# Attention scores, transposes and value products issued for two heads at a time

## Time and profile before

| | |
|---|---|
| median of 3 runs | 2915.23 us (2912.63 to 2915.69) |
| profiled execution | 2915.05 us |
| its span, first to last instruction | 2912.9 us |
| mean granted TensorE clock | 0.971 of full speed |
| busy: PE, PEld, DVE, ACT, POOL | 95%, 75%, 48%, 22%, 31% |

### The profile page before, as it was taken

One profiled execution on the slowest core, in us unless ns is written; L12 is line 12 of the kernel. 1 busy time (PEld: TensorE's weight loads), 2 busy tenths in 40 slices (PEclk: granted clock), 3 DMA queues, 4 the chain that ended last, 5 costly groups with the idle time before them and its releaser, 6 DMA issues.

```text
span 2912.9 us, 33971 instructions
## 1 busy us (share of the span) xinstructions
PE 2759.7 (95%) x12436; PEld 2198.0 (75%) x12436; DVE 1386.1 (48%) x2569; ACT 627.4 (22%) x1495; POOL 897.2 (31%) x870
## 2 busy tenths in 40 slices
PE   6799999999999999877999989998999999999997
PEld 2487778987789877765778767776787888888886
DVE  1421245986667676564346432223545344344346
ACT  3212222112321122441014022222122101101102
POOL 0531122432224232222424322222323343343343
PEclk8899999999999999997999989999999999999999
DMA  5410111122212132453334122223422111111113
GB/s 174 131 51 26 57 55 58 56 66 75 84 54 73 49 98 84 158 165 122 100 111 148 30 67 65 59 65 127 130 94 98 44 50 50 43 51 50 43 54 126
DMA packets 155596, 236.10 MB, mean 81 GB/s; under 512 B 24764, under 2 KB 69564, under 8 KB 155464
## 3 DMA queue, kind: packets, MB, share of 16 engines
q1 hardware_dynamic: 155464, 234.35, 25.3%
HBM read 181.65 MB, written 52.64 MB: 80 GB/s over the span
## 4 chain that ended last, share of the span: by engine, by line
PE 87%; DVE 8%; DMA 3%; ACT 1%; issue 1%; POOL 0%; SPq 0%; POOLq 0%; ACTq 0%; DVEq 0%
PE ps L1748 50%; PE ps L1895 12%; PE ps L1927 11%; PE ps L1806 5%; PE ps L1816 3%; PE ps L1830 3%; PE ps L1760 2%; PE ps L1777 2%; DVE act_lo L1239 1%; DVE scr L1326 1%; DMA small<-st_d 1%; DMA scr<-in_x 1%; DVE scr L1429 0%; DVE big L1669 0%; DVE big L1519 0%
## 5 line engine op out<-in xcount | busy, mean ns | idle before, releaser
L870 POOL CAST w_hi<-raw 128x512 fp32r<-128x512 f32 x416 | 306.0, 736 | 1948.5 <-DMA raw<-in_w_in 938.3
L1748 PE MATMUL ps<-act_hi,w_hi 128*128 128x512 f32 x1344 | 557.6, 415 | 48.4 <-DVE act_lo L1239 46.2
L872 POOL TENSOR_TENSOR w_lo<-raw,w_hi 128x512 fp32r<-128x512 f32 x416 | 580.3, 1395 | 33.3
L1748 PE MATMUL ps<-act_lo,w_hi 128*128 128x512 f32 x1344 | 532.6, 396 | 0.0
L1748 PE MATMUL ps<-act_hi,w_lo 128*128 128x512 f32 x1344 | 530.2, 394 | 0.0
L1326 DVE SCALAR_TENSOR_TENSOR scr<-scr,small 128x512 f32<-128x512 f32 x480 | 421.0, 877 | 11.5
L1748 PE MATMUL ps<-w_hi,act_hi 128*128 128x512 f32 (+1 forms) x960 | 387.4, 404 | 6.8 <-DVE act_lo L1239 6.5
L1748 PE MATMUL ps<-w_hi,act_lo 128*128 128x512 f32 (+1 forms) x960 | 376.0, 392 | 0.0
L1748 PE MATMUL ps<-w_lo,act_hi 128*128 128x512 f32 (+1 forms) x960 | 375.8, 391 | 0.0
L1748 PEld LDWEIGHTS ps<-act_hi,w_hi 128*128 128x128 f32 x1344 | 256.4, 191 | 102.2 <-issue 54.3
L1748 PEld LDWEIGHTS ps<-act_lo,w_hi 128*128 128x128 f32 x1344 | 255.6, 190 | 57.6
(11 more groups left out here) (173 smaller groups left out, 3113.5 us busy)
## 6 DMA issues: line engine op xcount, KB each, us to landing
raw<-in_w_in SPq DMA_DIRECT2D x176, 256.0 KB, 3.1
raw<-in_w_up SPq DMA_DIRECT2D x64, 256.0 KB, 2.7
raw<-in_w_down SPq DMA_DIRECT2D x64, 256.0 KB, 2.6
vreg<-in_w_ada SPq DMA_DIRECT2D x48, 256.0 KB, 3.5
raw<-in_w_in SPq DMA_DIRECT2D x72, 128.0 KB, 2.2
x_d<-big SPq DMA_DIRECT2D x16, 512.0 KB, 3.0
scr<-x_d SPq DMA_DIRECT2D x16, 512.0 KB, 4.2
o_d<-scr SPq DMA_DIRECT2D x48, 128.0 KB, 1.9
```

The source lines that it names most:

```text
L870: pool.tensor_copy(dhi, src).then_inc(w_hi_done, 1)
L872: pool.tensor_tensor(dlo, src, dhi.bitcast(F32), ALU.subtract).then_inc(w_ready, 1)
L1748: ins = nc.tensor.matmul(out_, lhs, rhs, start=(m == 0), stop=(m == 3 * nk - 1))
```

## The change

Two heads form a pair: heads 2i and 2i+1 of a block in groups 0 to 2, heads i and i+4 in group 3, always one on partitions 0 to 63 and one on 64 to 127. A group has 32 pairs and each does all its work within its own share of projection matmuls, 18 or 24 of them: 2 (3 in group 3) matmuls, both scores, 12 (15), all transposes of the pair into one bank, 4 (6), all value products of the pair into one bank. ScalarE copies the transposed probabilities of both heads in one instruction into the one buffer `probT`, VectorE both outputs in one. Counts of `probs_t`, `pt_out`, `pv` and `o_out` go by pairs. The taps of both steps come behind each other on VectorE, after both maxima. The cut diff (SyncE's two counts are halved alike; in group 3 VectorE's small steps for the sink, once a block, are put at pairs instead of steps):

```diff
+def pair_fill(C, p):
+
+    per = att_share(C)
+    a, b = 2 * p * per, 2 * p * per + 2 * per
+    return a, a + 2 * per // 8, b - 2 * per // 4, b
+
+
+def units_in(a, b):
+
+    return range(a // 24, b // 24)
+
-        probT = [scr[:, 512 + i * 256:512 + (i + 1) * 256] for i in range(2)]
+        probT = scr[:, 512:1024]
+        def pair_heads(g, p):
+
+            i = p % 4
+            return (2 * i, 2 * i + 1) if g < NG else (i, i + 4)
...
-            def probs_out(g, s):
-
-                a = 64 * g + s
-                n = att_cfg(g, s // 8)[1]
-                act.wait_ge(probs_t, a + 1)
-                if a >= 2:
-                    act.wait_ge(pv, a - 1)
-                nc.scalar.activation(probT[a % 2][:, 0:n], ps_t[:, 0:n], ACT.Copy
-                                     ).then_inc(pt_out, 1)
+            def probs_out(g, p):
+
+                n = att_cfg(g, p // 4)[1]
+                act.wait_ge(probs_t, 32 * g + p + 1)
+                if 32 * g + p >= 1:
+                    act.wait_ge(pv, 32 * g + p)
+                both = lambda t: t.rearrange("p (j k) -> p j k", j=2)[:, :, 0:n]
+                nc.scalar.activation(both(probT), both(ps_t), ACT.Copy).then_inc(pt_out, 1)
+
+            def att_pair(g, p):
+                us = att_units(g)
+                a, b, c, d = pair_fill(len(ATT_STAGES[g]), p)
+                for i in units_in(a, b):
+                    f_unit(us[i])
+                for j in range(2):
+                    exps(g, p, j)
+                for i in units_in(b, c):
+                    f_unit(us[i])
+                probs_out(g, p)
+                for i in units_in(c, d):
+                    f_unit(us[i])
...
-                B, h = s // 8, s % 8
+            def score_max(g, p, j):
+
+                B, h = p // 4, pair_heads(g, p)[j]
                 _, n, mask = att_cfg(g, B)
-                dve.wait_ge(scores, a + 1)
-                if a >= 2:
-                    dve.wait_ge(probs_t, a - 1)
-                nc.vector.tensor_tensor_reduce(prob[a % 2][:, 0:n], ps_s[a % 2][:, 0:n], mask, -0.125,
+                dve.wait_ge(scores, 64 * g + 2 * p + j + 1)
+                if 32 * g + p >= 1:
+                    dve.wait_ge(probs_t, 32 * g + p)
+                nc.vector.tensor_tensor_reduce(prob[j][:, 0:n], ps_s[j][:, 0:n], mask, -0.125,
                                                c_ns[:, h:h + 1] if g == 3 else 1e30, ALU.add, ALU.min,
                                                stat[:, B, h:h + 1]).then_inc(att_max, 1)
 
...
+            def out_pair(g, p):
+                B, i, a = p // 4, p % 4, 32 * g + p
                 dve.wait_ge(pv, a + 1)
-                src = ps_o[:, 0:HD]
+                src = ps_o[:, 0:2 * HD]
                 if g == 3:
-                nc.vector.tensor_copy(obuf[quad % 2][:, 64 * (h % 4):64 * (h % 4) + 64], src).then_inc(o_out, 1)
+                nc.vector.tensor_copy(obuf[quad % 2][:, P * (i % 2):P * (i % 2) + P], src).then_inc(o_out, 1)
...
             def attention(g):
                 us, C = att_units(g), len(ATT_STAGES[g])
                 if g >= 1:
                     dve.wait_ge(stat_st, 16 * (1, 3)[g - 1])
-                for s in range(66):
-                    if s < 64:
-                        score_max(g, s)
-                    if s >= 2:
-                        out_head(g, s - 2)
-                    if s < 64:
-                        for i in units_done(C, s):
-                            f_unit(us[i])
-                        if g < NG:
-                            conv_taps(("step", g, s))
+                for p in range(32):
+                    a, b, c, d = pair_fill(C, p)
+                    for i in units_in(a, b):
+                        f_unit(us[i])
+                    if p >= 1:
+                        out_pair(g, p - 1)
+                    for j in range(2):
+                        score_max(g, p, j)
+                    for i in units_in(b, d):
+                        f_unit(us[i])
+                    conv_taps(("step", g, 2 * p))
+                    conv_taps(("step", g, 2 * p + 1))
+                out_pair(g, 31)
...
-            def score(g, s):
-                a = 64 * g + s
-                B, h = s // 8, s % 8
+            def score_pair(g, p):
+                B = p // 4
                 k0, n, _ = att_cfg(g, B)
-                pair, half = (h // 2, h % 2) if g < 3 else (h % 4, h // 4)
-                rows = slice(64 * half, 64 * half + 64)
-                if a >= 2:
-                    pe.wait_ge(att_max, a - 1)
-                keys = kT[rows, pair, k0:k0 + n] if g < 3 else kT2[rows, k0:k0 + n]
-                nc.tensor.matmul(ps_s[a % 2][:, 0:n], qT[rows, pair, P * B:P * B + P], keys, start=True, stop=True
-                                 ).then_inc(scores, 1)
-
-            def prob_t(g, s):
-                a = 64 * g + s
-                n = att_cfg(g, s // 8)[1]
-                pe.wait_ge(probs, a + 1)
-                if a >= 1:
-                    pe.wait_ge(pt_out, a)
-                for i in range(n // P):
-                    ins = nc.tensor.transpose(ps_t[:, P * i:P * i + P],
-                                              prob[a % 2][:, P * i:P * i + P], ident[:, :])
+                if 32 * g + p >= 1:
+                    pe.wait_ge(att_max, 64 * g + 2 * p)
+                for j in range(2):
+                    rows = slice(64 * j, 64 * j + 64)
+                    keys = kT[rows, p % 4, k0:k0 + n] if g < 3 else kT2[rows, k0:k0 + n]
+                    nc.tensor.matmul(ps_s[j][:, 0:n], qT[rows, p % 4, P * B:P * B + P], keys, start=True, stop=True
+                                     ).then_inc(scores, 1)
+
+            def turn_pair(g, p):
+                n = att_cfg(g, p // 4)[1]
+                pe.wait_ge(probs, 64 * g + 2 * p + 2)
+                if 32 * g + p >= 1:
+                    pe.wait_ge(pt_out, 32 * g + p)
+                for j in range(2):
+                    for i in range(n // P):
+                        ins = nc.tensor.transpose(ps_t[:, 256 * j + P * i:256 * j + P * i + P],
+                                                  prob[j][:, P * i:P * i + P], ident[:, :])
                 ins.then_inc(probs_t, 1)
 
-            def prob_v(g, s):
-                a = 64 * g + s
-                B, h = s // 8, s % 8
-                k0, n, _ = att_cfg(g, B)
-                pe.wait_ge(pt_out, a + 1)
-                if a >= 1:
-                    pe.wait_ge(o_out, a)
-                for i in range(n // P):
-                    v = (V[:, k0 // P + i, 64 * h:64 * h + 64] if g < 3
-                         else V2[:, k0 // P + i, 64 * (h // 4):64 * (h // 4) + 64])
-                    ins = nc.tensor.matmul(ps_o[:, 0:HD],
-                                           probT[a % 2][:, P * i:P * i + P], v, start=(i == 0),
-                                           stop=(i == n // P - 1))
+            def value_pair(g, p):
+                k0, n, _ = att_cfg(g, p // 4)
+                pe.wait_ge(pt_out, 32 * g + p + 1)
+                if 32 * g + p >= 1:
+                    pe.wait_ge(o_out, 32 * g + p)
+                for j in range(2):
+                    h = pair_heads(g, p)[j]
+                    for i in range(n // P):
+                        v = (V[:, k0 // P + i, 64 * h:64 * h + 64] if g < 3
+                             else V2[:, k0 // P + i, 64 * (h // 4):64 * (h // 4) + 64])
+                        ins = nc.tensor.matmul(ps_o[:, HD * j:HD * j + HD],
+                                               probT[:, 256 * j + P * i:256 * j + P * i + P], v, start=(i == 0),
+                                               stop=(i == n // P - 1))
                 ins.then_inc(pv, 1)
 
             def attention(g):
 
-                us, per = att_units(g), att_share(len(ATT_STAGES[g]))
-                for s in range(66):
-                    if s < 64:
-                        for m in range(s * per, (s + 1) * per):
-                            proj(us[m // 24], m % 24)
-                        score(g, s)
-                    if 1 <= s < 65:
-                        prob_t(g, s - 1)
-                    if s >= 2:
-                        prob_v(g, s - 2)
+                us = att_units(g)
+                for p in range(32):
+                    a, b, c, d = pair_fill(len(ATT_STAGES[g]), p)
+                    for m in range(a, b):
+                        proj(us[m // 24], m % 24)
+                    score_pair(g, p)
+                    for m in range(b, c):
+                        proj(us[m // 24], m % 24)
+                    turn_pair(g, p)
+                    for m in range(c, d):
+                        proj(us[m // 24], m % 24)
+                    value_pair(g, p)
 
             for g in range(NG):
                 for u in STAGE_QKV[g]:
```

More of the change, by code:

```diff
@@ L1044, in _ @@
                     qkv_unit(u)
-                attention(g)
+                for p in range(32):
+                    att_pair(g, p)
             def ln_root(B):
```

(36 more changed lines are left out.)

47 lines of the change are left out of this document (13 added, 34 removed).

## The result

The changed kernel takes 2840.62 us (median of 4 runs, 2837.71 to 2843.49) against 2915.19 for the kernel before beside it: a ratio of 0.9746, with a 95% interval of 0.9729 to 0.9763.

A forecast was written before the change was run, and what follows sets the result against it. TensorE, busy 95% of the span, was taken as the bound, with time to win only between matmuls. Terms -11.3 - 7.9 - 13.7 + 2.2 + 2.0 = -28.7 us against 2915.05 gave 2886 us, range 2862 to 2905.

The forecast's parts named there:

- blocks rearranged, no overlap: TensorE's score, transpose and value blocks: a pair costs 2.80 instead of 2.88 us, or 1.70 instead of 1.80; -11.3 us.
- scores of a pair next to each other: TensorE's adjacent scores: the second head's first weight load goes under the first head's last record; 0.107 us a pair, -13.7 us.
- ends of the groups: Ends of attention groups on TensorE: the last block no longer drains two heads without fillers; -7.9 us.
- value products wait for the copy: TensorE ahead of value products: waits for ScalarE's copy of both heads' probabilities, 0.05 us for 44 pairs; +2.2 us.
- transposes wait for late maxima: TensorE ahead of transposes: VectorE's taps and gate unit delay the next pair's maxima by some 0.6 us; +2.0 us.
- The second head's weights: Step on a pair's neighbouring scores on different partition halves: one load hidden per pair, -13.7 us, bounds 0 and 35 us.
- What a score costs, and why: Step on score matmuls: each record pays 0.107 us of weight load besides its columns, 0.213 us at 256 keys.
- "no overlap" case: Rival for the paired scores: nothing overlaps between neighbouring scores, gain -15 us, 2900 us; chance 0.30.
- one record beside one record: Rival for the paired scores: second head's first record runs beside the first head's last, 35 us, giving 2865 us; chance 0.22.
- The block prices: Costs beyond fillers per pair on TensorE, 256 keys: scores 1.46, transposes 0.44, value products 0.90 us; 128 keys: 1.03, 0.22, 0.45.
- Rival 3: TensorE ahead of value products, groups 0 to 2: waits for the copy cost 27 us, slower at 2923 us; chance 0.07.

The follow-up runs named there:

- e2_same_half: Changed kernel with the second score of each pair also reading partitions 0 to 63, so the first head's scores are computed twice: 2883.87 us, ratio 0.9890.
- e5_cover2: Changed kernel with 2 instead of 4 projection matmuls (3 instead of 6 in group 3) between transposes and value products: 2873.27 us, ratio 0.9856.
- e4_taps_first: Changed kernel with VectorE's convolution taps of a pair's two steps put before that pair's gate products: 2833.69 us, ratio 0.9718.
- e7_before_halves: Kernel before with scores issued two by two and group 3's heads ordered 0, 4, 1, 5, ... so neighbours lie on different halves: 2828.60 us, ratio 0.9699.
- e1_split: Changed kernel with one projection matmul between the two scores of a pair, 11 behind them instead of 12: 2928.33 us, ratio 1.0042.

## Why the prediction was wrong

The sign was right and the size was not: -29 us forecast, -75 measured. Term by term, against the profiled span:

| term | forecast, us | measured, us |
|---|---|---|
| blocks rearranged, no overlap | -11.3 | -10.6 by its transposes and value blocks, with the scores at 1.46 and 1.03 |
| scores of a pair next to each other | -13.7 | 72 x (0.84 - 1.46) + 56 x (0.62 - 1.03) = -68 |
| ends of the groups | -7.9 | -8.8, the remainder |
| value products wait for the copy | +2.2 | in the first line, 0.02 a pair |
| transposes wait for late maxima | +2.0 | +10.1 |
| sum | -28.7 | -77.3 |

The remainder was not measured by itself. It holds one thing that the forecast didn't see: behind the drain of group 1 in the kernel before, in which TensorE stood for 0.75 and 0.98 us, the granted clock fell (third number from the end: 0.54 over this window, and 0.50 from 829 to 833; it is 1.00 on both sides).

```profile
827.00:834.50 7.50, 6.52 (x22) 5.44 (x21) 1.47 (x4) 0.38 (x1) 0.00 (x0) 0.54 0.35 87
```

Ten projection matmuls behind that drain start 0.43 us apart instead of 0.23, 2 us; the changed kernel has no drain there and a clock of 1.00.

**The step that failed is "The second head's weights".** It was wrong twice: in a price that it took over, and in its own bound.

First, in the price, which comes from the reading of rows 3, 4 and 6 under "What a score costs, and why". I divided the 0.32 us between a score's two records into 0.213 for columns and 0.107 for a weight load paid in each record. e2_same_half shows 0.32 only between the first and the second record of a block and 0.215 from there on. The first record is shown to start at its load (both at 300.98), so the difference of two starts held the load once; I charged it two more times for a pair. That is 25 us in the "no overlap" case, which should have been 2875 us and not 2900. The trace of before could have told: a score's last record was 0.31 us from the next transposes, which is 0.213 and a change of mode, and I took it for the same 0.32.

Second, in what neighbours on different halves do. I took one weight load under one matmul (0.107 us a pair) from the transposes' rows, and bounded the term at one record beside one record, 35 us, because I let the second head's first record start no earlier than the first head's second. In the profile the first records of both heads start together, then the second ones: the first head's second record doesn't stand in the way. Nothing in the trace of before showed two matmuls at once, so the bound had to be the full second score, 0.64 and 0.42 us, 70 us for 128 pairs. I named that value nowhere, and with it in place of the 35 us the low end of the range would have been near 2827, below the measured time. The rule of the Trainium skill that I quoted for this rival, that different tiles load and multiply in parallel ("TensorEngine Tiling (Array Packing)", Key Properties), is borne out in full: the pair's block costs 0.84 us, a lone score's 0.82 (1.46 less the 0.64 of two records). I had let a lesser price stand for it. What one sentence of the Trainium skill says of weight loads on the page "TensorE: Matmul & The Clock Gate", Part 3, that they overlap matmuls in flight only where the row group differs, does not hold here: in e2_same_half the loads of one half are hidden under matmuls of the same half.

**The block prices held.** Transposes 0.44 and 0.22, value products 0.92 and 0.44 (forecast 0.90 and 0.45). **The copy's wait** was level as forecast: TensorE's weight load waits for the copy in 44 cases, 0.19 us each, and the matmuls lose 0.02.

```profile
PEld ps L1852 <- ACT scr L1045: 8.5, 44, 0.2
```

**The late maxima** had the right mechanism and the wrong size. Groups 1 and 2 have seven stalls, 7.4 us together, up to 1.8 us each and not 0.6; six of them (5.6 us) follow a gate product as foreseen. I had left out that VectorE waits for ScalarE's tanh before it begins that product, with the taps standing in its queue behind it. Another 2.7 us are at the start of group 3, where the first transposes stand nearer to a VectorE that waits for a DMA.

**Rival 3** (slower by the copy's wait) fell as its own arithmetic of where units end had it: no weight load of the value products waits longer than 0.2 us. e5_cover2 shows that its wait comes with two fillers less, 0.47 us a pair; even then the kernel is not slower than the kernel before. Its share for a tanh was not met in the changed kernel.

What the change is worth by parts, from the runs: putting the scores next to each other on different halves, -88 us (2828.6 against 2916.7 beside it, in the kernel before with nothing else). All the rest of the change costs 12 us (9.8 between the profiled spans, 2835.6 and 2825.9). By the starts in the two traces that is three things. Stalls ahead of the transposes are 13 us against 4, of which e4_taps_first takes 5 away by the order on VectorE. The three blocks of a pair cost 0.84 + 0.44 + 0.92 = 2.20 us against 2.13 for the two in e7_before_halves (2.17 against 2.12 in group 3, 1.29 against 1.25 with 128 keys), 7 us together. The remainder is 6 us the other way, and fits the drains at the ends of the groups, which e7_before_halves still has. The last two were read from the traces and not tried by themselves.

## What to carry to other kernels

Two fp32 matmuls that contract over 64 partitions each and stand next to each other in TensorE's queue, on different halves, cost the time of one here (0.84 us for two heads, 0.82 for one); one other matmul between them loses all of it (88 us in e1_split). All pairs here write into different banks, so what a common bank would do is not shown. Look for this in the order of the queue before any regrouping of the work around it: three lines that move an issue gave as much as the rewrite by pairs (2842.7 and 2840.6 us), and with the heads of group 3 in another order 12 us more. And when a trace doesn't show an operation side by side with its like, bound the gain by the whole of the second one, not by the part that a neighbouring row suggests.

## What the runs showed of the hardware that was not expected

- Two fp32 scores on different halves: both first records start within 0.01 us of each other, both second ones too; four records are 0.70 us long, as two were. The second head costs about 0.02 us.
- In the 64-row mode a weight load on the same half is hidden behind the matmul before it (records 0.215 us apart at 256 keys). The block as a whole costs about 0.41 us beyond its columns (0.84 us, less 2 x 0.215; with 128 keys 0.62, less 2 x 0.107), where four transposes cost 0.01 (0.44, less 4 x 0.107).
- The first matmul behind a change between 128 and 64 rows is shown to start with its weight load (the score at 300.98 in e2_same_half, as its load), so the first distance in a block of scores is longer than the others by that load: 0.32 us against 0.215.
